# The boundary between two transformer blocks on one core: row tile by row tile, with the weight splits of the next units behind the last row's chain

## What is computed

```python
# end of the first block (y_a, y_b are its two gated halves, each with its own RMS norm)
out = _rmsnorm(concat([y_a, y_b]) @ w_out, g_post)
x1  = x + gate * out
# start of the second block
h    = rms_norm(x1, norm_gain) * (1 + scale) + shift
proj = h @ w_in                       # q, k, v, z for each pair of heads
...
x    = x1 + gate_2 * (concat([oa, ob]) @ w_out_2)
```

## Time and profile before

| | us |
|---|---|
| median of 3 runs | 2897.68 |
| the three runs | 2896.97, 2897.68, 2900.3 |
| the profiled execution's own time | 2896.28 |
| its span in the profile | 2894.5 |
| TensorE busy in the span | 2833.1 (98%) |
| VectorE busy | 1481.4 (51%) |
| ScalarE busy | 1008.3 (35%) |
| POOL busy | 360.2 (12%) |

### The profile page before, as it was taken

One profiled execution on the slowest core, in us unless ns is written; L12 is line 12 of the kernel. 1 busy time (PEld: TensorE's weight loads), 2 busy tenths in 40 slices (PEclk: granted clock), 3 DMA queues, 4 the chain that ended last, 5 costly groups with the idle time before them and its releaser, 6 DMA issues. The chain is left out here.

```text
span 2894.5 us, 36817 instructions
## 1 busy us (share of the span) xinstructions
PE 2833.1 (98%) x15014; PEld 2369.6 (82%) x15014; DVE 1481.4 (51%) x1760; ACT 1008.3 (35%) x1344; POOL 360.2 (12%) x411
## 2 busy tenths in 40 slices
PE   6999999999999999999999999899999999999999
PEld 2678888888889998888888888688888888888787
DVE  6868678755565456666652333623343344333532
ACT  7742222234334332433332322323343343222311
POOL 1011101001233313341210000100000000000000
PEclk8999999999999999999999999899999999999999
DMA  9657667654545554555555433232222222222342
GB/s 398 222 185 257 244 242 276 244 182 137 176 146 153 164 173 141 165 168 162 153 181 183 131 103 101 103 109 73 73 81 81 73 81 89 86 88 88 117 153 95
DMA packets 162135, 439.58 MB, mean 152 GB/s; under 512 B 14768, under 2 KB 59824, under 8 KB 151728
## 3 DMA queue, kind: packets, MB, share of 16 engines
q1 hardware_dynamic: 123360, 307.28, 33.5%
q0 software_dynamic: 15792, 92.99, 9.1%
q10 hardware_dynamic: 22816, 36.97, 3.7%
HBM read 398.11 MB, written 39.06 MB: 151 GB/s over the span
## 5 line engine op out<-in xcount | busy, mean ns | idle before, releaser
L1449 DVE TENSOR_TENSOR WL<-RAW,WH 128x1024 fp32r<-128x1024 f32 (+1 forms) x424 | 515.4, 1224 | 839.9 <-ACT WH L936 634.0
L397 PE MATMUL PB<-HH,WH 128*128 128x512 f32 x2048 | 822.4, 402 | 8.8 <-DVE WL L1449 5.6
L402 PE MATMUL PB<-HL,WH 128*128 128x512 f32 x2048 | 805.5, 393 | 0.0
L403 PE MATMUL PB<-HH,WL 128*128 128x512 f32 x2048 | 805.2, 393 | 0.0
L936 ACT ACTIVATE WH<-RAW 128x1024 fp32r<-128x1024 f32 (+1 forms) x424 | 432.1, 1038 | 462.8 <-PE PB L521 208.4
L397 PEld LDWEIGHTS PB<-HH,WH 128*128 128x128 f32 x2048 | 387.3, 189 | 98.7 <-issue 15.0
L403 PEld LDWEIGHTS PB<-HH,WL 128*128 128x128 f32 x2048 | 387.4, 189 | 67.6
L402 PEld LDWEIGHTS PB<-HL,WH 128*128 128x128 f32 x2048 | 387.7, 189 | 65.7 <-issue 3.4
L519 PE MATMUL PB<-WH,HH 128*128 128x512 f32 x768 | 300.1, 391 | 2.9 <-DVE evb L1449 1.5
L521 PE MATMUL PB<-WH,HL 128*128 128x512 f32 x768 | 299.6, 390 | 0.0
L520 PE MATMUL PB<-WL,HH 128*128 128x512 f32 x768 | 299.6, 390 | 0.0
(11 more groups left out here) (298 smaller groups left out, 3155.7 us busy)
## 6 DMA issues: line engine op xcount, KB each, us to landing
RAW<-in_w_in_t SPq DMA_DIRECT2D x320, 512.0 KB, 3.7
AU<-in_w_ada POOLq DMA_DIRECT2D x64, 1024.0 KB, 5.6
RAW<-in_w_out_t SPq DMA_DIRECT2D x96, 512.0 KB, 3.6
bcb<-R SPq DMA_DIRECT2D x64, 256.0 KB, 5.9
S<-so ACTq DMA_DIRECT2D x24, 384.0 KB, 2.7
ebc<-R SPq DMA_DIRECT2D x32, 256.0 KB, 6.2
SY<-evb ACTq DMA_DIRECT2D x32, 256.0 KB, 2.2
yin<-SY POOLq DMA_DIRECT2D x32, 256.0 KB, 4.0
```

Source lines behind the costliest of these rows:

```text
L397: h.matmul(banks[j], lh, m.HH[:, t, :], start=st, stop=False)
L402: h.matmul(banks[j], lh, m.HL[:, t, :], start=False, stop=False)
L403: ins = h.matmul(banks[j], ll, m.HH[:, t, :], start=False, stop=en)
L1449: return h.tensor_tensor(o, a, b, op)
```

## The change

It touches block 7 of the output product, everything between it and the first projection units, and nothing else.

- TensorE, block 7: units kk = 0 to 3 run as before. The matmuls of kk = 4 to 7 are put in another order, row tile by row tile: for k = 0 all four units, then for k = 1, and so on. Bank k is announced after its own 24 matmuls.
- VectorE, ScalarE and POOL: each row tile gets its own chain (`take_out`, `gain_out`, `make_x1`, `sum_x1`, `scale_x1`; `square_out`, `square_x1`, `scale_x1`), written interleaved so that a row's later steps stand among the next row's first ones. x1 and its squares go by halves of 1024 channels. POOL makes `rx` and `rx2` for each row in turn.
- The scaled identity matrices go. Instead x1 times 1/rms is written to `m.XR` (`xs2`: the first 1024 channels by ScalarE, the last 1024 by VectorE), and TensorE turns that with `h.transpose` against the plain identity.
- TensorE turns rows 0 to 2 of channel tiles 0 to 3 before it comes to row 3.
- The splits of units AT_IN2 and AT_IN2 + 1 stand behind row 3's chain in both programs, the 4 MB DMA behind them on ScalarE.
- In `modulate2` the odd tiles' `h2` move from VectorE to ScalarE (an Identity activation with scale and bias). One `next` runs ahead of the first projection unit, so t = 0 to 5, and the conversion of `m.exact` stands behind it.

The diff, without the removed buffers' neighbourhood:

```diff
@@ -210,7 +210,7 @@
     m.ra, m.rb, m.rv = sm(4), sm(4), sm(4)
-    m.ss2, m.A2 = sm(24), sm(16)
+    m.ss2, m.xsq, m.A2 = sm(24), sm(8), sm(16)
     m.rc, m.vm, m.qgs, m.onec = sm(16), sm(8), sm(1), sm(1)
@@ -317,10 +317,6 @@
     m.jk, o = mem("jk", [128, 512], o)
-    m.dg2 = []
-    for k in range(4):
-        x, o = mem(f"dgb{k}", [128, 128], o)
-        m.dg2.append(x)
@@ -761,7 +757,7 @@
-            for kk in range(8):
+            for kk in range(8 if i < 7 else 4):
                 o_unit(AT_OUT + 8 * i + kk, kk, banks, ready, i)
@@ -774,13 +770,38 @@
+    for k in range(4):
+        for kk in range(4, 8):
+            n = AT_OUT + 56 + kk
+            split_ready(n)
+            wh = m.WH[n % 4].rearrange("p (t c) -> p t c", t=2)
+            wl = m.WL[n % 4].rearrange("p (t c) -> p t c", t=2)
+            for tt in range(2):
+                t = 2 * kk + tt
+                ready(t)
+                xh, xl = m.HH[:, t, k * 128:(k + 1) * 128], m.HL[:, t, k * 128:(k + 1) * 128]
+                h.matmul(banks[k], xh, wh[:, tt, :], start=False, stop=False)
+                h.matmul(banks[k], xh, wl[:, tt, :], start=False, stop=False)
+                ins = h.matmul(banks[k], xl, wh[:, tt, :], start=False, stop=t == 15)
+            if k == 3:
+                ins.then_inc(*put(s.unit, "used", n))
+            elif kk == 7:
+                ins.then_inc(*put(s.block, "out", 7, k))
+    def turn_row(t, bank, k):
+        P.wait_ge(*at("xs2", k, t // 8))
+        return h.transpose(bank[:, k * 128:(k + 1) * 128], m.XR[:, k, t * 128:(t + 1) * 128], ident)
     def modulate2():
+        first = [take(hb, "turn2", t) for t in range(4)]
+        for t, (b, bank) in enumerate(first):
+            for k in range(3):
+                turn_row(t, bank, k)
         for t in range(16):
-            b, bank = take(hb, "turn2", t)
-            for k in range(4):
-                P.wait_ge(*at("dg2", k))
-                ins = h.matmul(bank[:, k * 128:(k + 1) * 128], m.O[:, k, t * 128:(t + 1) * 128], m.dg2[k],
-                               start=True, stop=True)
+            b, bank = first[t] if t < 4 else take(hb, "turn2", t)
+            for k in range(3 if t < 4 else 0, 4):
+                ins = turn_row(t, bank, k)
             ins.then_inc(*put(P.side, "turn2", t))
@@ -890,7 +911,6 @@
     m2 = modulate2()
-    next(m2)
     next(m2)
@@ -1244,7 +1264,8 @@
                 u = AT_OUT + 8 * i + kk
-                make(u + 2)
+                if u + 2 < AT_IN2:
+                    make(u + 2)
                 for L in halves_due(i, kk):
@@ -1263,7 +1284,7 @@
                     A.then(act(dst, m.PB[4 * (i % 2) + k], ACT.Copy, scale=m.ra[:, k:k + 1]), "O", i, k)
-                else:
+                elif nb < 3:
                     A.wait_ge(*at("O", i, k))
@@ -1271,15 +1292,41 @@
                                   "O squared", nb, k)
-    for k in range(4):
-        A.wait_ge(*at("x1", k))
-        A.then(act(m.XR[:, k, :], m.O[:, k, :], ACT.Square, acc=m.ss2[:, 20 + k:21 + k]), "x1 squared", k)
+    def square_out(k):
+        A.wait_ge(*at("O", 7, k))
+        A.wait_ge(*(at("O squared", 3, k - 1) if k else junk))
+        A.then(act(m.jk, m.O[:, k, 1536:2048], ACT.Square, acc=m.ss2[:, k * 4 + 3:k * 4 + 4]), "O squared", 3, k)
+    def square_x1(k):
+        for half in range(2):
+            sl = slice(1024 * half, 1024 * half + 1024)
+            A.wait_ge(*at("x1", k, half))
+            A.then(act(m.XR[:, k, sl], m.O[:, k, sl], ACT.Square, acc=m.xsq[:, 2 * k + half:2 * k + half + 1]),
+                   "x1 squared", k, half)
+    def scale_x1(k):
+        A.wait_ge(*at("rx2", k))
+        A.wait_ge(*at("x1 squared", k, 0))
+        A.then(act(m.XR[:, k, 0:1024], m.O[:, k, 0:1024], ACT.Copy, scale=m.ss2[:, 20 + k:21 + k]), "xs2", k, 0)
+    square_out(0)
+    square_x1(0)
+    square_out(1)
+    scale_x1(0)
+    square_x1(1)
+    square_out(2)
+    scale_x1(1)
+    square_x1(2)
+    square_out(3)
+    scale_x1(2)
+    square_x1(3)
+    scale_x1(3)
+    make(AT_IN2)
+    make(AT_IN2 + 1)
     h.dma_start(m.XD.rearrange("k p c -> p k c"), m.O).then_inc(*land(s.XD, "XD"))
-    A.wait_ge(*at("cst"))
-    for n in m.exact:
-        t = A.then(act(m.exact[n], m.C(n), ACT.Copy), *(("exact",) if n == "triS" else ()))
@@ -1287,6 +1334,14 @@
                 A.then(act(m.HH[:, t - 1, :], m.yin[(t - 1) % 3], ACT.Copy), "HH2", t - 1)
+            if t < 16 and t % 2:
+                A.wait_ge(*at("turn2", t))
+                A.wait_ge(*at("A2"))
+                if t >= 3:
+                    A.wait_ge(*at("HH2", t - 3))
+                    A.wait_ge(*at("HL2", t - 3))
+                A.then(act(m.yin[t % 3], bank("turn2", t), ACT.Identity, scale=m.A2[:, t:t + 1],
+                           bias=m.mod2[:, t:t + 1]), "h2", t)
             if t in (5, 9, 13):
@@ -1370,7 +1425,9 @@
     next(m2)
-    next(m2)
+    A.wait_ge(*at("cst"))
+    for n in m.exact:
+        A.then(act(m.exact[n], m.C(n), ACT.Copy), *(("exact",) if n == "triS" else ()))
     bg = deque([m2])
@@ -1836,7 +1893,8 @@
             for kk in range(8):
-                make(AT_OUT + 8 * i + kk + 2)
+                if AT_OUT + 8 * i + kk + 2 < AT_IN2:
+                    make(AT_OUT + 8 * i + kk + 2)
                 for L in halves_due(i, kk):
@@ -1848,7 +1906,7 @@
                 V.then(h.tensor_copy(m.rb, bank("gate sums")[:, 0:4]), "rb sum")
-            if half == 0:
+            if half == 0 or nb == 3:
                 continue
@@ -1858,34 +1916,77 @@
                 dst = m.O[:, k, sl]
-                if nb == 3 and k == 2:
-                    V.wait_ge(*at("O squared", 3, 3))
-                    V.then(h.tensor_reduce(m.ss2[:, 16:20], m.ss2[:, 0:16].rearrange("p (k n) -> p k n", k=4), AXX,
-                                           ALU.add), "rx sum")
                 V.wait_ge(*at("O squared", nb, k))
                 V.wait_ge(*at("gg"))
-                t = V.then(TT(dst, dst, m.gg[:, sl], ALU.mult), "Og", nb, k)
+                V.then(TT(dst, dst, m.gg[:, sl], ALU.mult), "Og", nb, k)
+    def take_out(k):
+        dst = m.O[:, k, 1536:2048]
+        V.wait_ge(*(at("out", 7, k) if k < 3 else at("used", AT_OUT + 63)))
+        V.wait_ge(*at("O", 3, k))
+        V.then(STT(dst, m.PB[4 + k], m.rb[:, k:k + 1], dst, ALU.mult, ALU.add), "O", 7, k)
+    def gain_out(k):
+        dst = m.O[:, k, 1536:2048]
+        V.wait_ge(*at("O squared", 3, k))
+        V.then(h.tensor_reduce(m.ss2[:, 16 + k:17 + k], m.ss2[:, 4 * k:4 * k + 4], AXX, ALU.add), "rx sum", k)
+        V.then(TT(dst, dst, m.gg[:, 1536:2048], ALU.mult), "Og", 3, k)
+    def make_x1(k):
+        V.wait_ge(*at("rx", k))
+        V.wait_ge(*at("XR", k))
+        for half in range(2):
+            sl = slice(1024 * half, 1024 * half + 1024)
+            V.wait_ge(*at("Og", 1 + 2 * half, k))
+            V.then(STT(m.O[:, k, sl], m.O[:, k, sl], m.ss2[:, 16 + k:17 + k], m.XR[:, k, sl], ALU.mult, ALU.add),
+                   "x1", k, half)
+    def sum_x1(k):
+        V.wait_ge(*at("x1 squared", k, 0))
+        V.wait_ge(*at("x1 squared", k, 1))
+        V.then(TT(m.ss2[:, 20 + k:21 + k], m.xsq[:, 2 * k:2 * k + 1], m.xsq[:, 2 * k + 1:2 * k + 2], ALU.add),
+               "rx2 sum", k)
+    def scale_x1(k):
+        V.wait_ge(*at("rx2", k))
+        V.then(TS(m.XR[:, k, 1024:2048], m.O[:, k, 1024:2048], m.ss2[:, 20 + k:21 + k], None, ALU.mult), "xs2", k, 1)
     V.then(STT(m.A2, m.mod2[:, 16:32], 1.0, m.P("ng2"), ALU.add, ALU.mult), "A2")
-    V.wait_ge(*t)
-    for k in range(4):
-        V.wait_ge(*at("rx"))
-        V.wait_ge(*at("XR", k))
-        V.then(STT(m.O[:, k, :], m.O[:, k, :], m.ss2[:, 16 + k:17 + k], m.XR[:, k, :], ALU.mult, ALU.add), "x1", k)
-    for k in range(4):
-        V.wait_ge(*at("rx2", k))
-        V.then(TS(m.dg2[k], m.C("ident"), m.ss2[:, 20 + k:21 + k], None, ALU.mult), "dg2", k)
-    t = V.then(TS(m.qgs, m.P("qg"), float(1.0 / np.sqrt(128)), None, ALU.mult), "qgs")
+    V.then(TS(m.qgs, m.P("qg"), float(1.0 / np.sqrt(128)), None, ALU.mult), "qgs")
     V.then(h.memset(m.onec, 1.0), "one")
+    take_out(0)
+    gain_out(0)
+    make_x1(0)
+    take_out(1)
+    sum_x1(0)
+    gain_out(1)
+    scale_x1(0)
+    make_x1(1)
+    take_out(2)
+    sum_x1(1)
+    gain_out(2)
+    scale_x1(1)
+    make_x1(2)
+    take_out(3)
+    sum_x1(2)
+    gain_out(3)
+    scale_x1(2)
+    make_x1(3)
+    sum_x1(3)
+    scale_x1(3)
+    make(AT_IN2)
+    make(AT_IN2 + 1)
...
                 v = t - 2
+                V.wait_ge(*at("h2", v))
                 V.wait_ge(*at("HH2", v))
                 V.then(TT(m.HL[:, v, :], m.yin[v % 3], m.HH[:, v, :].bitcast(F32), ALU.subtract), "HL2", v)
-            if t < 16:
+            if t < 16 and t % 2 == 0:
                 V.wait_ge(*at("turn2", t))
@@ -2191,10 +2291,10 @@
         y_load(L)
-    G.wait_ge(*at("rx sum"))
-    mean_power(m.ss2[:, 16:20], 2048, "rx")
     for k in range(4):
-        G.wait_ge(*at("x1 squared", k))
```

(3 more changed lines are left out.)

## The result

| | before | changed | |
|---|---|---|---|
| median, run by turns on one chip (7 executions each) | 2898.65 | 2889.96 | ratio 0.997, 95% interval 0.9957 to 0.9983 |
| profiled execution's own time | 2896.28 | 2888.02 | 8.26 less |
| forecast | | 2889.3 | range 2885.5 to 2894.5 |

A forecast was written before the change was run, and what follows sets the result against it. TensorE, busy 98% of the span, bounds the kernel, leaving its waits to win. Boundary terms put the third projection unit at T + 34.7 against 43.1, gain 8.4 us: 2887.9 profiled, 2889.3 median, range 2885.5 to 2894.5.

The forecast's parts named there:

- Pitch of the chains: From one row's `O` to the next: 6.0 to 6.1 us, while TensorE delivers a row every 5.45.
- POOL at 1.4 for `rx`: In each row's chain, POOL's `rx` pair takes 1.4 us, as it meets the 0.68 of `Og`.
- POOL held by VectorE at all: VectorE operations with two SBUF inputs lock POOL out of the shared ports; without it the gain is 1.4 us larger.
- Row 3 behind T: The last row's chain after block 7's last matmul (T): `O` at T + 1.5, ScalarE's scaling done at 11.1.
- Splits behind the chain: The two weight splits moved between row 3's scaling and the first `h2` cost 3.4 us.
- Turning rows 0 to 2 ahead: 12 transposes in TensorE's wait before row 3, worth about 1.3 us, already in the first unit's T + 17.5.
- Clock: TensorE's clock, down after the boundary: 3.5 us of the first projection unit at half speed, 1.75 us lost.
- Transposes at 0.11: Turning by one-piece transposes at 0.11 us each: 40 for tiles 6 to 15 put 4.4 us on the path.
- POOL is not held: Rival, chance 0.17: POOL pairs take 0.9 us everywhere, the chain keeps up with TensorE, gain 9.8 us.
- The clock stays down through the first unit: Rival, chance 0.12: with transposes before and behind it, the first unit takes 11.2 us; gain 4.6, 2893.1 us.
- Handoffs: Rival, chance 0.11: some 14 semaphore steps behind T cost 0.2 us more than 0.04 each; gain 5.6 us.
- Slower, POOL held each time: Rival, chance 0.05: VectorE stretches POOL's pairs to 4.4 us each time, a loss of 7.1, 2904.8 us.

The follow-up runs named there:

- e11: The changed kernel run once more with no edit; median 2890.05 us against 2899.45 before, ratio 0.9964.
- e4: Changed kernel with row chains interleaved otherwise: second square and scaling behind the next row's first steps, POOL's `rx` ahead of the former row's `rx2`; 2889.12 us, ratio 0.9968.
- e3: Changed kernel with AT_IN2's split moved into row 3's chain and AT_IN2 + 1's behind the first six tiles; 2886.99 us, ratio 0.9955 to the kernel before.
- e2: Changed kernel without turning rows 0 to 2 ahead of row 3; 2891.46 us, ratio 0.9974 to the kernel before.
- e7: Changed kernel with 19 unread float32 matmuls of 128x512 added around the turning; 2893.11 us, ratio 0.9983 to the kernel before.
- e6: Changed kernel with tiles 0 to 9 turned ahead of the first unit, instead of 0 to 5; 2889.96 us, ratio 0.9969 to the kernel before.
- e1: Changed kernel with the last four units of block 7 unit by unit again; 2903.45 us, ratio 1.0014 to the kernel before.
- e10: Kernel before with only block 7's last four units row by row and the two splits behind the scaled identities; 2898.77 us, ratio 0.9999.
- e8: e3 and e4 together, with VectorE's scalings of rows 2 and 3 later and turning ahead row by row; 2884.62 us, ratio 0.996 to the kernel before.
- e9: e8 with 27 unread float32 matmuls of 128x128 in TensorE's waits; 2882.6 us, ratio 0.9941 to the kernel before.

## Why the prediction was right, step by step

The mechanism was as forecast and the sum came out within 0.2 us. Part of that closeness is luck: small errors cancelled, and the clock came back where the forecast had it in this execution, but 1.3 us earlier in e11, which gives a fourth unit at 39.7 and a gain of 9.0. Between 8.4 and 9.0 one profile can't decide.

- **Announcement of the rows.** Rows 0 and 1 are taken at T - 16.12 and T - 10.68 (forecast T - 16.3 and T - 10.9). Right, and row 0's cover held: no stall inside block 7.
- **Pitch of the chains**, 6.0 to 6.1: measured 6.16. Row 3's `O` at T + 1.64, forecast 1.5. Right.
- **POOL at 1.4 for `rx`**: mis-sized by 0.3, by a term that was not in the sum. The pair itself is 1.22; what stretched it was the scaling of the row before, not `Og`, as I had written: beside `Og` (1839.71 to 1840.39) the first operation took its 0.20. But row 3's reduce ends at 1839.80 and its x1 starts at 1841.49, 1.69 later, since POOL was still at row 2's `rx2` until 1840.16. It is a place in POOL's queue that I had not priced, not VectorE's hold alone. e4, which puts `rx` first, shows what it was worth.
- **POOL held by VectorE at all**: right in kind. The Trainium skill, "SBUF — State Buffer", section "Who interferes with whom", names both of the VectorE operations met here as able to contend with GpSimd, a `tensor_scalar` and one with two SBUF inputs; it spells out that the pair is held for the whole instruction beside the fast two-port modes only, and that the operation with two inputs does the same is my reading of its rule of one exclusive lock. The traces agree as far as they go: the scaling on VectorE stretched POOL's operation from 0.54 to 0.93, and x1 beside it gave 1.29 and 1.46 in e4.
- **Row 3 behind T**: scaling done at T + 11.42, forecast 11.1. The halves of x1 were 2.48 (2.5 forecast), the square 1.06 with 0.19 for its sum, ScalarE's scaling 1.15 (1.1). VectorE's scaling was 0.75, not 0.65.
- **Splits behind the chain**, 3.4: from row 3's scaling to `h2` 3.33 passed, but without the splits `h2` would have come 0.56 behind the scaling all the same (e3: 11.43 and 11.99), for it needs the turning. Their price is 2.8. Mis-sized by 0.6, with no effect on the forecast.
- **Turning rows 0 to 2 ahead**, "worth about 1.3, already in the 17.5": wrong. e2 shows 0. The splits hid the turning; the two terms cannot both be counted. It did no harm to the sum, which had only the later of the two on the path.
- **First unit** at T + 17.7, forecast 17.5. Its length with the clock down, 7.32 (1853.79 to 1861.11), forecast 7.35. **Clock**: 1.75 forecast, 1.77 measured against e7; but 1.19 in e11, so the match to 0.02 is luck.
- **Transposes at 0.11**: 0.104 in the dense stretch. The prediction set 4.4 us for 40 of them against 5.2 for the 48 pieces of before, and so hid that the halved pieces carry a good part of the gain (the estimate of 4.5 us above). Third unit at T + 33.91, forecast 33.9.
- **The 4 MB copy beside the weight loads**: landed in 13.9 us where it took 13.1, and no weight load was waited for. Cost 0, right.
- **The rivals.** *POOL is not held*: refuted, by 0.93 in place of 0.54. *The clock stays down through the first unit*: refuted in the changed kernel; the premise, that transposes leave the clock alone, is refuted by e6. *Handoffs*: the sum came out with 0.04 each, so there is no room for 0.2 more; no run measures them alone. *Slower, POOL held each time*: not so here, as x1 follows `rx` by its data. A slower kernel did exist one edit away, in e1, and it was not the one I had named: the same kernel without the early rows loses 2.8 us.

From the DMA issues of the changed kernel (KB each, median us to landing), the copy of x1:

```profile
XD<-O ACTq DMA_DIRECT2D x1, 4096.0 KB, 13.9
```

## What to carry to other kernels

Where a serial stage follows a product, order the product's last units so that a part of its output is finished early, and build the stage's chain per part: the early rows alone gave nothing (e10), all the rest of the change without them lost (e1), both together took 8.4 us off. The cheaper turning had a share in this, estimated above and not tested by itself. Then read which engine's list stands between the chain and the next product; the work that had to be moved behind the chain is the next thing to place, and here the right places (e8) were worth 4.8 us more by the traces. With gains near a measurement's scatter, measure from a landmark inside the trace, and count two hidden things once: what lies behind a longer wait is worth nothing until that wait goes.

## What the runs showed of the hardware

- Transposes alone brought TensorE's clock back from 0.50 to 1.00 (e6, between 1867 and 1868, ahead of the first other matmul). With small float32 matmuls in the gaps it never fell (e9, 1.00 in every window of 1 us from T to T + 42), where it fell to 0.50 within T + 6 in every other kernel here.
- With the same code, the clock's fall (T + 4.5, T + 3.1) and its return (T + 21.5, T + 20.2) both moved by 1.3 us between two executions, while the first `h2` and the first unit repeated to 0.01.
- A float32 matmul of 512 columns is two pieces of 0.44 us, 0.89 in all (e7), where one with fp32r operands starts every 0.23.
- POOL's two operations on 128 x 1 take 0.19 and 0.54 when VectorE is idle (row 3's `rx2` of the changed kernel). Beside VectorE's 128 x 1024 scaling the second took 0.93, beside two 128 x 1024 operations with two inputs the pair took 1.29 and 1.46 (e4): each ran out only after the VectorE operation beside it.
